# Seven block products in place of eight for the gate and half of the output of a hybrid layer, with weight sums made by accumulating transfers

## What is computed

```python
proj = x @ w_in                       # split: q, k, v, z_attn, z_ssm, xbc, dt
attn = sliding_window_attention(q, k, v, sinks) * silu(z_attn)
xbc  = silu(causal_depthwise_conv(xbc))
y    = ssd_chunked(xs, dt, a, bm, cm) + xs * d_skip       # state space, 2 chunks of 128
ssm  = gated_rmsnorm(y, z_ssm)                             # y * silu(z_ssm), normed
out  = concat([attn, ssm]) @ w_out
x    = layer_norm(ALPHA * x + out) * ln_g + ln_b
```

## Time and profile before

| | |
|---|---|
| median of 3 runs | 1930.42 us (1927.97 to 1931.52) |
| the profiled execution | 1933.01 us, its span 1930.7 us |
| mean granted TensorE clock | 0.914 |
| TensorE matmul busy | 1570.6 us, 81% of the span |
| VectorE, ScalarE, GpSimd busy | 680.6, 303.6, 13.0 us |
| moved by the transfer engines | 554.44 MB, mean 287 GB/s |

### The profile page before, as it was taken

One profiled execution on the slowest core, in us unless ns is written; L12 is line 12 of the kernel. 1 busy time (PEld: TensorE's weight loads), 2 busy tenths in 40 slices (PEclk: granted clock), 3 DMA queues, 4 the chain that ended last, 5 costly groups with the idle time before them and its releaser, 6 DMA issues.

```text
span 1930.7 us, 21893 instructions
## 1 busy us (share of the span) xinstructions
PE 1570.6 (81%) x9530; PEld 949.8 (49%) x9530; DVE 680.6 (35%) x1393; ACT 303.6 (16%) x802; POOL 13.0 (1%) x39
## 2 busy tenths in 40 slices
PE   9999999999999999766565657555665656799999
PEld 7775567755699995222222222212222212357886
DVE  2663455634486863311111111101111111144533
ACT  1343313432122102000000000000000000213220
POOL 0000000000000000000000000000000000000000
PEclk9999999999999999988777877788787888899999
DMA  9851377414244456999999999999999999954300
GB/s 378 282 148 46 113 266 220 131 51 166 97 164 142 175 219 262 423 431 432 429 432 430 432 429 429 432 418 433 430 429 431 431 431 430 369 195 168 126 13 22
DMA packets 87784, 554.44 MB, mean 287 GB/s; under 512 B 4512, under 2 KB 11424, under 8 KB 74112
## 3 DMA queue, kind: packets, MB, share of 16 engines
q1 hardware_dynamic: 86544, 548.81, 70.9%
q0 software_dynamic: 1136, 4.10, 0.6%
HBM read 551.85 MB, written 1.05 MB: 286 GB/s over the span
## 4 chain that ended last, share of the span: by engine, by line
PE 60%; DMA 35%; DVE 4%; ACT 1%; issue 1%; POOL 0%; SPq 0%; DVEq 0%; ACTq 0%; POOLq 0%
PE bank L677 27%; DMA ring<-in_w 22%; DMA arena<-in_w 13%; PE bank L1155 8%; PE bank L704 7%; PE bank L686 6%; PE bank L1183 3%; PE bank L665 3%; PE bank L1468 1%; PE bank L876 1%; PE bank L809 1%; PE bank L789 1%; DVE arena L2404 0%; PE bank L1126 0%; PE bank L1206 0%
## 5 line engine op out<-in xcount | busy, mean ns | idle before, releaser
L1155 PE MATMUL bank<-ring,arena 128*32 128x512 f32 x1216 | 287.2, 734 | 147.7 <-DMA arena<-in_w 97.7
L677 PE MATMUL bank<-arena,ring 128*128 128x128 f32 (+1 forms) x2528 | 393.7, 315 | 0.5 <-DVE arena L3073 0.5
L677 PEld LDWEIGHTS bank<-arena,ring 128*128 128x128 f32 x2528 | 357.2, 191 | 30.8 <-issue 7.1
L1155 PE MATMUL bank<-arena 128*32 128x512 f32 x832 | 231.6, 728 | 104.0 <-DMA ring<-in_w 97.4
L677 PE MATMUL bank<-ring,arena 128*128 128x512 f32 (+3 forms) x520 | 205.2, 544 | 1.7 <-DVE ring L2419 0.8
L1155 PEld LDWEIGHTS bank<-ring,arena 128*32 128x32 f32 x1216 | 73.1, 132 | 269.0 <-issue 269.0
L1155 PEld LDWEIGHTS bank<-arena 128*32 128x32 f32 x832 | 56.6, 131 | 189.3 <-issue 189.1
L1183 PE MATMUL bank<-ring,arena 128*32 128x512 f32 x576 | 122.2, 663 | 23.0 <-DMA arena<-in_w 15.2
L677 PEld LDWEIGHTS bank<-ring,arena 128*128 128x128 f32 x520 | 96.1, 190 | 84.1 <-issue 72.3
L704 PE MATMUL bank<-ring,arena 128*128 128x512 f32 (+1 forms) x320 | 129.0, 560 | 2.1 <-DMA ring<-in_w_vd 1.1
L1183 PE MATMUL bank<-arena 128*32 128x512 f32 x384 | 98.9, 674 | 21.7 <-DMA ring<-in_w 21.7
(11 more groups left out here) (395 smaller groups left out, 1465.8 us busy)
## 6 DMA issues: line engine op xcount, KB each, us to landing
ring<-in_w SPq DMA_DIRECT2D x53, 4096.0 KB, 31.6
arena<-in_w SPq DMA_DIRECT2D x35, 4096.0 KB, 37.7
ring<-in_w_in SPq DMA_DIRECT2D x40, 2048.0 KB, 8.3
ring<-in_w_mod SPq DMA_DIRECT2D x6, 2048.0 KB, 12.9
ring<-in_w_out SPq DMA_DIRECT2D x6, 2048.0 KB, 7.8
arena<-in_w SPq DMA_DIRECT2D x6, 2048.0 KB, 11.1
ring<-in_w SPq DMA_DIRECT2D x6, 2048.0 KB, 11.6
ring<-in_w_out SPq DMA_DIRECT2D x16, 512.0 KB, 9.3
```

Source lines behind the costliest of these rows:

```text
L677: i = te.matmul(ps, lhsT, rhs, start=n0 + k == 0, stop=n0 + k == n - 1)
L1155: m = te.matmul(ps[32 * j:32 * j + 32, :], LM.xg[:, f, 128 * k + 32 * j:128 * k + 32 * j + 32], vs[j][:, 512 * (k % 2):512 * (k % 2) + 512 ...
```

## The change

The host makes one more input, `w_quads`: for each layer the gate's and the output's 1024x1024 weights, cut into four quadrants of 512x512 (column half, row half), each laid out as 128 partitions of 2048 numbers. A product of 256x1024 by 1024x1024 is then computed as a 2x2 by 2x2 block product with seven block products (`layer_seven`), each four matmuls of 512 columns: products 1, 2 and 7 take token blocks as they are, 3 to 6 take sums of token blocks (`layer_token_sums`, four VectorE operations into a region that was the layer norm gains'). The weight sums are made in the ring by transfers on POOL's queue that add to their destination: a third buffer, `T`, is loaded with two quadrants for each of `zs` and `oa`, and four accumulating transfers of 1 MB each make the first, third (sources in HBM), second and fourth sum (sources in the ring). The seven products stand in seven of the eight places, in banks 4 to 7 in turn; the eighth place holds nothing on TensorE. All other strands have banks 0 to 3 already from place 32.

VectorE joins the parts: for the gate into halves in the arena, with ScalarE taking the tanh from there; for the output straight into `h`. `out_ssm` then starts banks of its own, and `norm_sums` adds them without the scaling. The first product of each seven is copied out by ScalarE. The norm gains are loaded behind the last accumulating transfer and product 6 of the output. The ring's first turn is 1 instead of 5, so that the mixer finds the same buffers.

```diff
-            turn, in_turn = [5], list(range(NR))
+            turn, in_turn = [1], list(range(NR))
...
-                for g in range(2):
-                    layer_load(("zs", ly, g), (whole, wv[:, :, 2560 + 512 * g:3072 + 512 * g]))
-                for n in range(2):
-                    ns = slice(512 * n, 512 * n + 512)
-                    layer_load(("oa", ly, n), *[(lambda v, a=a, kp=kp: v[64 * a:64 * a + 64, 4 * kp:4 * kp + 4, :],
...
+                load_quadrants(("zs", ly, 0), 0, 0)
+                load_quadrants(("zs", ly, 1), 0, 2)
+                load_quadrants(("T", "zs", ly), 0, 2)
+                load_quadrants(("oa", ly, 0), 1, 0)
+                load_quadrants(("T", "oa", ly), 1, 2)
+                load_quadrants(("oa", ly, 1), 1, 2)
...
+            def layer_seven(name, ly, xT):
...
+                def times(k, x, w):
+                    ps = fresh("P", name, ly, k, b=4 + ((k - 1) if name == "zs" else k + 6) % 4)
+                    product(ps[:, :], [(x[:, c, :], w[:, c, :]) for c in range(4)]).then_inc(*t.done("mm", "P", name, ly, k))
+                t.wait_ge(*at.of("w", (name, ly, 0)))
+                times(1, xT[:, 0:4, lo], w0[:, 0:4, :])
+                yield
+                times(2, xT[:, 4:8, lo], w0[:, 4:8, :])
+                yield
+                ready(("w", (name, ly, 1)), ("S", name, ly))
+                times(3, S[3], w1[:, 4:8, :])
+                yield
+                ready(("T", name, ly, 1), ("T", name, ly, 2))
+                times(4, S[1], T[:, 4:8, :])
+                yield
+                times(5, S[0], T[:, 0:4, :])
+                yield
+                ready(("T", name, ly, 3))
+                times(6, S[2], w1[:, 0:4, :])
+                t.also("used", (name, ly, 1))
+                yield
+                ready(("T", name, ly, 4))
+                times(7, xT[:, 4:8, hi], w0[:, 4:8, :])
...
-                for g in range(2):
-                    t.wait_ge(*at.of("w", ("zs", ly, g)))
-                    for tt in range(2):
-                        yield from tok512(("zs", ly, tt, g), hT, weights(("zs", ly, g)), tt)
...
                 banks.width = 4
+                yield from layer_seven("zs", ly, hT)
+                yield
                 ready(*[("ev", "pv", ly, n) for n in range(4)])
...
+                yield from layer_seven("oa", ly, L1.zaT)
+                yield
...
+                def gate_tanh(tt, g):
+                    to = scratch(("zs", ly, tt, g), 512)
+                    ready(("half", "zs", ly, tt, g))
+                    se.activation(to, L1.zs[:, tt, 512 * g:512 * g + 512], ACT.Tanh).then_inc(*a.done("ev", "zs", ly, tt, g))
+                conv_tanh(CONV[-1])
+                ready(("mm", "P", "zs", ly, 1), ("S", "zs", ly))
+                se.mul(L1.part, bank("P", "zs", ly, 1)[:, :], 0.5).then_inc(*a.done("ev", "P", "zs", ly, 1))
+                for gate in (None, None, None, (0, 0), None, (0, 1), (1, 1), (1, 0)):
+                    if gate is not None:
+                        gate_tanh(*gate)
+                    yield
+                ready(("mm", "P", "oa", ly, 1), ("ev", "P", "zs", ly, 7))
+                se.copy(L1.part, bank("P", "oa", ly, 1)[:, :]).then_inc(*a.done("ev", "P", "oa", ly, 1))
...
+                    if n == 8:
+                        layer_token_sums("zs", ly, hT)
...
+            def layer_gate_sums(ly):
...
+                yield
+                yield
+                ready(("ev", "P", "zs", ly, 1))
+                half(0, 0, 2, X, ALU.add)
+                yield
+                to_part(X, 4, 0.5, X).then_inc(*v.done("ev", "P", "zs", ly, 4))
+                gate(0, 0)
+                yield
+                ready(("mm", "sc", ly, 3, 1))
+                to_part(Y, 5, -0.5, X).then_inc(*v.step())
+                half(0, 1, 3, Y, ALU.subtract)
+                yield
+                to_part(X, 6, 0.5, X).then_inc(*v.done("ev", "P", "zs", ly, 6))
+                half(1, 1, 5, X, ALU.subtract)
+                gate(0, 1)
+                yield
+                half(1, 0, 7, X, ALU.add)
+                gate(1, 1)
+                yield
+                gate(1, 0)
+                layer_token_sums("oa", ly, L1.zaT)
+                yield
...
+            def layer_out_sums(ly):
...
+                def residual(tt, g, k, other, op):
+                    hv = h[:, tt, 512 * g:512 * g + 512]
+                    behind()
+                    ve.scalar_tensor_tensor(hv, hv, ALPHA, other, ALU.mult, op).then_inc(*v.step())
+                    ready(("mm", "P", "oa", ly, k))
+                    behind()
+                    ve.tensor_tensor(hv, bank("P", "oa", ly, k)[:, :], hv, ALU.add).then_inc(*v.done("ev", "P", "oa", ly, k))
+                yield
+                yield
+                ready(("ev", "P", "oa", ly, 1))
+                residual(0, 0, 2, X, ALU.add)
+                yield
+                to_part(X, 4, ALU.add).then_inc(*v.done("ev", "P", "oa", ly, 4))
+                yield
+                to_part(Y, 5, ALU.subtract, flip=True).then_inc(*v.step())
+                residual(0, 1, 3, Y, ALU.subtract)
+                yield
+                to_part(X, 6, ALU.add).then_inc(*v.done("ev", "P", "oa", ly, 6))
+                residual(1, 1, 5, X, ALU.subtract)
+                yield
+                residual(1, 0, 7, X, ALU.add)
+                yield
+                yield
...
-                ve.scalar_tensor_tensor(hv, hv, ALPHA, P[4 + 2 * tt + n][:, :], ALU.mult, ALU.add
+                ve.tensor_tensor(hv, hv, bank("o", ly, tt, n)[:, :], ALU.add
...
-                ready(("mm", "k", ly, 0), *([("h", 0, 0), ("h", 0, 1)] if ly else []))
+                for name, k in (("zs", 1), ("zs", 3), ("zs", 2), ("oa", 1), ("zs", 4), ("oa", 2), ("oa", 3), ("oa", 4)):
...
+                    if k == 1:
+                        ready(("w", ("T", name, ly)))
+                        dst, src = T[:, 0, :], quads[0]
+                    elif k == 2:
+                        ready(("T", name, ly, 1))
+                        dst, src = T[:, 1, :], T[:, 0, :]
+                    elif k == 3:
+                        ready(("w", (name, ly, 1)))
+                        dst, src = w1[:, 0, :], quads[3]
+                    else:
+                        ready(("T", name, ly, 2), ("T", name, ly, 3), ("mm", "P", name, ly, 2))
+                        dst, src = w0[:, 1, :], T[:, 1, :]
+                    ge.dma_start(dst, src, accum_op=ALU.add).then_inc(*summed[k - 1].inc())
+                    at.put(("T", name, ly, k), summed[k - 1].sem, summed[k - 1].n)
+                ready(("mm", "P", "oa", ly, 6), ("T", "oa", ly, 4))
```

More of the change, by code:

```diff
@@ L237, in program @@
         ada_c_sem = sem("ada_c_loaded")
+        summed_sem = [sem(f"weights_summed{k}") for k in range(4)]
         h_sem = [sem(f"h{tt}_loaded") for tt in range(2)]
@@ L306, in program @@
             lng, lnb = ar(22848, 1024), ar(23872, 1024)
+            sums = [ar(22848 + 512 * k, 4, 128) for k in range(4)]
+            part, part1 = ar(22336, 512), ar(6144, 512)
             y = ar(17464, 2, 1024)
@@ L2132, in layer_proj @@
                         conv_gated(CONV[n - 1])
+                    if n == 8:
+                        layer_token_sums("zs", ly, hT)
                     yield
[L2134 to L2142 removed]
+                conv_gated(CONV[-1])
@@ new lines, in layer_proj, with layer_token_sums @@
+                yield from layer_gate_sums(ly)
+                yield from layer_out_sums(ly)
+            def layer_token_sums(name, ly, xT):
+                lo, hi = slice(0, 128), slice(128, 256)
+                s1, s2, s3, s4 = L1.sums
+                behind()
+                if name == "oa":
+                    ready(("mm", "P", "zs", ly, 6))
+                ve.tensor_tensor(s1, xT[:, 0:4, hi], xT[:, 4:8, hi], ALU.subtract).then_inc(*v.step())
+                ve.tensor_tensor(s3, xT[:, 0:4, lo], xT[:, 0:4, hi], ALU.subtract).then_inc(*v.step())
+                behind()
+                ve.tensor_tensor(s2, s1, xT[:, 0:4, lo], ALU.subtract).then_inc(*v.step())
+                behind()
+                ve.tensor_tensor(s4, xT[:, 4:8, lo], s2, ALU.add).then_inc(*v.done("S", name, ly))
@@ new lines, in layer_gate_sums, with to_part, half, gate @@
+            def layer_gate_sums(ly):
+                X, Y = L1.part, L1.part1
+                def to_part(dst, k, scale, other, op=ALU.add):
+                    ready(("mm", "P", "zs", ly, k))
+                    behind()
+                    return ve.scalar_tensor_tensor(dst, bank("P", "zs", ly, k)[:, :], scale, other, ALU.mult, op)
+                def half(tt, g, k, other, op):
+                    to_part(L1.zs[:, tt, 512 * g:512 * g + 512], k, 0.5, other, op).then_inc(*v.done("ev", "P", "zs", ly, k))
+                    v.also("half", "zs", ly, tt, g)
+                def gate(tt, g):
+                    gated(("zs", ly, tt, g), L1.zs[:, tt, 512 * g:512 * g + 512], 512)
```

(28 more changed lines are left out.)

53 lines of the change are left out of this document (16 added, 37 removed).

## The result

The changed kernel takes 1944.15 us in the median (1942.44 to 1945.25), beside 1930.97 (1927.97 to 1933.22) of the kernel before on the same chip: a ratio of 1.0069, 95% interval 1.0056 to 1.0081. It is 13 us slower, where 1932.5 us was forecast and 1941 was the upper end. The profiled execution has a span of 1942.6 us, 11.9 more than before.

What follows compares the result with a forecast made beforehand. TensorE was taken as the bound in block 1, the transfer engines half idle. Terms -13.8 - 0.7 + 15.8 + 0.8 = +2.1 us gave 1932.5 us on the median, range 1920 to 1941.

Steps and rivals of the forecast that it cites:

- What goes: Gate and output: seven products instead of eight places, 6.9 us a layer less on TensorE, 13.8 us for both.
- the tanh wait: First layer: a 0.7 us wait for the tanh goes, since the bank of the output's first product is drained earlier.
- VectorE's and ScalarE's additions: Each layer: 26 more VectorE operations, 18 us, fitting by volume; ScalarE loses four copies, gains two; costed at nothing.
- (a): At the gate, B's transpose waits for VectorE to read the value product's bank: 0.8 us a layer.
- (b): Gate's empty eighth place: two decay matrices back to back, so the first small products wait 2.4 us a layer.
- (c): After the gate: last gating and output's token sums on VectorE delay the next small products by 0.8 us a layer.
- (d): Output's empty eighth place: a chain of 8.9 us against TensorE's 5.2; last small products wait 3.7 to 3.9 us.
- Waits: New waits of TensorE in the layers' gate and output places: 7.9 us a layer, 15.8 us in all.
- Transfers: Extra loads on SP's queue, eight 1 MB accumulating transfers on POOL's: about 12 us each, hidden.
- The rival of a late fourth sum: Product 7 waits on the accumulating transfer, costing from 21 us on; at 30 us, 1958 us total; chance 0.13.
- The rule that the prediction quotes for that rival: POOL's transfers need descriptors that GpSimd writes; VectorE's two-port instructions lock it out; no size given.
- The rival that the gain survives: Block 1: VectorE and ScalarE hand over sooner, waits shrink to half or less; 1916 to about 1925 us; chance 0.27.

Runs made afterwards that it cites:

- the last kernel: Changed kernel with the seven products spread over eight places, late pieces mended, and the bank counter set at each layer's end to the changed kernel's: 1920.33 us, ratio 0.9941.
- experiment 8: Changed kernel with the seven products spread three and four matmuls to a place, late token sums, tanh and copy moved, banks rechosen: 1926.71 us, ratio 0.9974.
- experiment 4: Changed kernel with both empty places moved ahead of the gate's products, later pieces one or two places later: 1951.62 us, ratio 1.0106.
- experiments 6 and 7: Both against the changed kernel. 6: two matmuls in each empty place, 1936.47 us. 7: seven products spread three and four matmuls over eight places, 1934.69 us.

## Why the prediction was wrong

**What goes** was right: 32 records, 13.8 us, and the tanh wait.

**VectorE's and ScalarE's additions** were nearly right at nothing on their own. With the places filled, and all of the sums present, the time is within 0.1% of before, but 2.7 us of that are the layer's end; in the two layers' stretches 1.9 and 3.0 us are left, (a), the bank wait, and 0.2 and 0.6 us of the chain.

**Waits.** (a) 0.8 forecast, 0.80. (b) 2.4, 2.78 in both layers. (c) 0.8, none. The half clock behind (b) gives the chain that much more time. With the gate's place filled 0.22 us of it shows, and with the place half filled, behind a stand of 1.05 us at full clock, 0.63 in both layers; how much there would be at full clock behind the whole stand is not shown. (d) 3.7 to 3.9, 4.03. The sum forecast was 7.9 a layer; measured 8.3, with a wait of 0.69 for a bank of the turned probabilities that the replay did not have. So the sum of this part, on which most of the working was spent, was within 0.4 us, in part because the 0.8 that did not come and the 0.69 that was not foreseen cancel.

**The step that failed** is the sentence on what a stand costs besides its length: "Each restart also shows a first weight load, 0.1 us, eight times: 0.8." It prices every matmul behind a stand at its duration at full clock. The first weight load is there, 1.97 us behind a stand against 1.89 without one, but besides it the runs show 12.8 us, in the first layer 6.3 for two stands. Replaced by that figure, and with the 0.7 in place of (c), the sum is -13.8 - 0.7 + 16.6 + 12.8 = +14.9 us, less 2.2 between the layers: 12.7, as the stretches give it. No rival held it either, since all of them kept the price of a matmul. The earlier trace rows gave the clock as 1.00 in four stretches, and I read that as a property of the stage; it was a property of a TensorE that hardly stood. The one longer stand of block 1, 1.96 us at 250.19, lay outside the four stretches, with 5.78 us behind it where 4.19 is full clock. The -2.2 us between the layers, which brought the time nearer to the forecast, was in no term of it.

The range failed for the same reason: its upper end of 1938 to 1941 was built from longer waits and a late transfer, each in microseconds of waiting.

The Trainium skill has the mechanism (TensorE: Matmul & The Clock Gate, "HAM oscillation — how this bites in real kernels"): a TensorE that waits between short bursts is throttled again each time, and its matmuls run slow until the clock is given back. The traces here agree, with 1.97 us for sixteen records of small products at full clock and 3.65 at half. It is a rule that bore on this change, and the prediction weighed two others.

**Transfers** were right: 12 us taken, 10.7 in the median, all hidden, and without them the same time. The rival of a late fourth sum was wrong: the four fourth sums took 7.1, 7.1, 7.5 and 6.9 us, and the longest of all sixteen transfers 18.4. The rule that the prediction quotes for that rival from the Trainium skill (SBUF — State Buffer, "SBUF: two separate sides") cost nothing that a run here shows. By the rule on the adding transfer's rate, also from the Trainium skill (Collectives: The Full Stack, "The bandwidth ceiling", told there of ReduceScatter), a megabyte was estimated at about 8 us; the fourth sums are a little under that, the median is over it, and how busy the engines were differs too much for a verdict.

**The rival that the gain survives** was wrong for this kernel and right for this product scheme: spread over the places, the seven products bring about 9.4 of the 10.2 us by which the last kernel is faster, of the 14.5 that this rival allowed at best. What it needed was no faster VectorE but matmuls left beside the chain's links. That the spread kernel could reach this was not in the prediction.

## What to carry to other kernels

When work is taken off the bounding engine, ask of each place from which it is taken how long the other engines' chain beside it is; take it where the chain is short, or a little from every place, not a whole place at once. Price a stand of TensorE of more than some 2 us at its length plus about 3 us for the matmuls behind it at half clock, which was the mean of the four such stands of the changed kernel and nearly doubled the cost of the waits. And a counter that hands out banks is shared: change it in one stage, and set it back behind it, or a wait appears, or goes, in a stage that the diff does not touch. Read the whole trace of before for stands, not at the stages of the change alone: the one at 250 us showed the price.

## What the hardware showed beyond that

The small products behind a stand are a gauge of the clock: 1.97 to 2.00 us at full, 3.65 at half, with values between where the clock changed under them. They miss a fall that comes later, so the third column says what the granted clock did. Over all traces, the stands of a microsecond or more in the two layers that small products ended:

| stand, us | small products behind, us | half clock followed |
|---|---|---|
| 1.05 to 1.13 (eight) | 1.97 to 2.00 | once, as they ended (experiment 8) |
| 1.42 | 2.00 | no |
| 2.19 to 2.32 (six) | 3.65, 3.65, 3.28, and three times 1.97 | four times, once only behind them |
| 2.77 to 2.78 (six) | 3.56, 3.24, 2.89, 2.75, 2.20 and 3.59 | six times |
| 2.95 (two) | 3.65, 3.65 | twice |
| 4.03 to 4.04 (six) | 3.41, and five times 3.65 | six times |

The late fall among the 2.2 us is in the second layer of experiment 4: the clock fell 3 us behind that stand, while TensorE stood for another 1.41 us. The other stands of 2.4 us or more in block 1 and the mixer (2.42 twice, 2.52, 3.15 twice, 3.43 twice) were all followed by half clock. The stand of 1.96 us in the first layer's end is in five traces, and in one of them, that of the kernel before, the clock fell. The mixer's two stands of some 1.6 and 1.7 us were followed by full clock in all traces.

So a stand of 1.0 to 1.4 us was free behind it in eight of nine cases, and none of the 21 of 2.4 us or more was. Between them both happen: at 1.96 us with the same work around the stand in five kernels, and at 2.2 to 2.3 us in the two layers of experiments 6 and 7, the first layer one way and the second the other. What else than the length decides stays open. With one trace of each kernel, no run shows how often the clock falls behind one and the same stand.
